# The first stage of a two-layer block on one core: tiles mixed in two pairs and kept in SBUF, two rows broadcast by TensorE

## The reference, cut to what matters

```python
def first_block(...):
    sh1, sc1, g1, sh2, sc2, g2 = split(silu(c) @ ada_w + ada_b)      # 1024 -> 6*1024
    u = rms_norm(x, mix_pre_g) * (1 + sc1) + sh1
    y = concat([(window_mean(u_g, w) - u_g) @ pool_w[g] for g, w in enumerate((2, 4, 8, 16))]) * pool_scale
    x = x + g1 * rms_norm(y, mix_post_g)
    u = rms_norm(x, ffn_pre_g) * (1 + sc2) + sh2
    f = conv_ffn(u, w_up, conv_w, conv_b, w_down)
    return x + g2 * rms_norm(f, ffn_post_g)
```

## Time and profile before

| | us |
|---|---|
| median of three runs | 1283.73 |
| profiled execution, its own time | 1283.86 |
| its span | 1282.0 |
| PE busy | 1216.9 (95% of the span) |
| first product of the up units starts | 93.53 |
| product 49, the first of the second unit, starts | 106.82 |
| DVE, ACT, POOL busy | 551.5, 520.3, 378.6 |

### The profile page before, as it was taken

How to read it: one execution, slowest core, us unless ns; L and a number is a source line. 1 busy time by engine, 2 the same in 40 slices (tenths; PEclk the granted TensorE clock), 3 DMA queues, 4 the chain that set the end, 5 groups by cost and what they waited for, 6 DMA issues and landing times.

```text
span 1282.0 us, 16325 instructions
## 1 busy us (share of the span) xinstructions
PE 1216.9 (95%) x6572; PEld 1019.9 (80%) x6572; DVE 551.5 (43%) x853; ACT 520.3 (41%) x669; POOL 378.6 (30%) x92
## 2 busy tenths in 40 slices
PE   5989999999899989999999999999999699999986
PEld 5568878888788867888788978888888479999874
DVE  1464344343722253558854357422100632453714
ACT  4254543445411145654343324644312544335523
POOL 0014433444434433224221120044444124233111
PEclk9889999999999989999999999999999789999998
DMA  9993223222322232223322112032322313222101
GB/s 352 386 323 106 92 83 98 95 91 90 109 94 99 99 125 73 66 50 116 99 66 67 34 33 99 1 93 72 131 99 99 106 33 99 67 66 67 65 1 66
DMA packets 108206, 128.48 MB, mean 100 GB/s; under 512 B 13019, under 2 KB 98785, under 8 KB 108017
## 3 DMA queue, kind: packets, MB, share of 16 engines
q1 hardware_dynamic: 103412, 120.69, 28.2%
q10 hardware_dynamic: 4733, 6.91, 1.6%
HBM read 122.35 MB, written 5.24 MB: 100 GB/s over the span
## 4 chain that ended last, share of the span: by engine, by line
PE 45%; DVE 3%; ACT 1%; issue 1%; DVEq 0%; ACTq 0%
PE ps L242 11%; PE ps L244 11%; PE ps L243 11%; PE ps L1482 2%; PE ps L2064 2%; PE ps L1821 1%; PE ps L1829 1%; PE ps L1858 1%; PE ps L1949 1%; PE ps L1955 1%; PE ps L1950 1%; PE ps L1931 1%; DVE xres L1377 1%; PE ps L2083 1%; DVE xres L1367 0%
## 5 line engine op out<-in xcount | busy, mean ns | idle before, releaser
L364 POOL TENSOR_TENSOR wl<-raw,wh 128x2048 fp32r<-128x2048 f32 x81 | 374.4, 4622 | 875.3 <-ACT wh L389 875.3
L242 PE MATMUL ps<-xth,wh 128*128 128x512 f32 x800 | 321.2, 401 | 3.9 <-DVE xtl L974 3.2
L244 PE MATMUL ps<-xth,wl 128*128 128x512 f32 x800 | 313.6, 392 | 0.0
L389 ACT ACTIVATE wh<-raw 128x2048 fp32r<-128x2048 f32 x81 | 154.9, 1912 | 390.5 <-PE ps L244 390.5
L243 PE MATMUL ps<-xtl,wh 128*128 128x512 f32 x800 | 313.0, 391 | 0.0
L242 PEld LDWEIGHTS ps<-xth,wh 128*128 128x128 f32 x800 | 151.4, 189 | 36.5 <-issue 6.7
L244 PEld LDWEIGHTS ps<-xth,wl 128*128 128x128 f32 x800 | 151.0, 189 | 32.5
L243 PEld LDWEIGHTS ps<-xtl,wh 128*128 128x128 f32 x800 | 151.6, 190 | 29.1
L242 PE MATMUL ps<-wh,xth 128*128 128x256 f32 (+1 forms) x320 | 98.8, 309 | 3.4 <-DVE xtl L867 3.4
L243 PE MATMUL ps<-wl,xth 128*128 128x256 f32 (+1 forms) x320 | 98.0, 306 | 0.0
L244 PE MATMUL ps<-wh,xtl 128*128 128x256 f32 (+1 forms) x320 | 97.8, 306 | 0.0
(11 more groups left out here) (287 smaller groups left out, 1733.1 us busy)
## 6 DMA issues: line engine op xcount, KB each, us to landing
ada<-in_ada_w SPq DMA_DIRECT2D x24, 1024.0 KB, 10.6
raw<-in_gdn_w_in SPq DMA_DIRECT2D x24, 1024.0 KB, 5.1
raw<-in_ffn_w_up SPq DMA_DIRECT2D x22, 1024.0 KB, 5.0
raw<-in_gla_w_in SPq DMA_DIRECT2D x12, 1024.0 KB, 5.0
raw<-in_ffn_w_down SPq DMA_DIRECT2D x11, 1024.0 KB, 4.8
raw<-in_gdn_w_out SPq DMA_DIRECT2D x8, 1024.0 KB, 4.9
raw<-in_gla_w_out SPq DMA_DIRECT2D x4, 1024.0 KB, 5.0
xres<-in_x SPq DMA_DIRECT2D x4, 512.0 KB, 5.2
```

The source lines that it names most:

```text
L242: nc.tensor.matmul(o, lh, rh, start=first, stop=False)
L244: return nc.tensor.matmul(o, ll, rh, start=False, stop=last)
L364: nc.gpsimd.tensor_tensor(wl[:, s, :], raw[:, s, :], wh[:, s, :].bitcast(f32), ALU.subtract)\
L389: nc.scalar.activation(wh[:, s, :], raw[:, s, :], ACT.Copy).then_inc(hi_done, 1)
```

## The change

- The rows `pool_scale` and `mix_post_g` are loaded to one partition (`scale_rows`, 4 KB each, at the head of SP's program) in place of 512 KB each. PE spreads them with four products of a column of ones (one partition, 512 columns each) into banks 0 to 3, placed after the turned rows and ahead of the band sums; ACT copies them to `pool_scale_row` and `post1_row`, ahead of the squares of x. The first `ada_unit` waits for these copies. The band matrices are stored three times in place of four (864 KB in place of 1152 KB).
- `mixed` takes two tiles at once, the pair 0 and 1 and then the pair 2 and 3; the second pair waits only for ACT's new copy of y to SBUF (`y_copied`), and comes ahead of all four units of group 3.
- ACT's program: for each of the four tiles the squares, the copy and the root of y; then for each tile the squares, root and `xn` of u. DVE's program: `norm` of y no longer adds to x; `mixed_in(tt)` does that from the SBUF copy, with g1. They stand in the order that the diff shows.
- `mod_cols` with scale are computed with the gain multiplied in first.
- ACT makes the high part from `pooled` itself, with scale and shift (Identity), and waits only for `mods_done` and the four turned tiles; DVE computes the same value to a ring of four and subtracts, block by block.
- The first up unit goes block by block, both chunks in each block (`first_unit`): six products for each low part.

```diff
-NORM_ORDER = (("y", 0), ("y", 1), ("u", 0), ("y", 2), ("u", 1), ("y", 3), ("u", 2), ("u", 3))
+NORM_ORDER = tuple((what, tt) for what in "yu" for tt in range(TT))
+BAND_OF = (0, 1, 1, 2)
...
-    pool_band = at("pool_band", PH + 40 * KB, [POOL_GROUPS, TT, BAND])
+    pool_band = at("pool_band", PH + 40 * KB, [POOL_GROUPS, TT - 1, BAND])
+    scale_rows = at("scale_rows", PH + 16 * KB, [2, D])
+    y_early = at("y_early", PH + 24 * KB, [2, D])
+    y_late = at("y_late", PH + 40 * KB, [2, D])
+    u_ring = at("u_ring", PH + 24 * KB, [4, T])
...
+        def y_of(tt):
...
+            return (y_early if tt < 2 else y_late)[:, tt % 2, :]
...
+            sp.dma_start(scale_rows[0:1, 0, :], a["pool_scale"][0].rearrange("(a n) -> a n", a=1)).then_inc(S("ident_in"), 16)
+            sp.dma_start(scale_rows[0:1, 1, :], a["mix_post_g"][0].rearrange("(a n) -> a n", a=1)).then_inc(S("ident_in"), 16)
...
-            sp.dma_start(pool_scale_row[:], a["pool_scale"][0].partition_broadcast(P)).then_inc(S("pool_in"), 16)
...
-            sp.dma_start(post1_row[:], a["mix_post_g"][0].partition_broadcast(P)).then_inc(S("post_in"), 16)
...
+            act.wait_ge(S("rows_turned"), 2)
+            nc.scalar.activation(pool_scale_row[:], bank2(2), ACT.Copy).then_inc(S("c_silu"), 1)
+            nc.scalar.activation(post1_row[:], bank2(0), ACT.Copy).then_inc(S("c_silu"), 1)
...
-            norm_square("y", 0)
-            norm_root("y", 0)
-            norm_square("y", 1)
-            norm_root("y", 1)
-            norm_square("u", 0)
-            norm_square("y", 2)
-            norm_root("u", 0)
-            norm_root("y", 2)
-            norm_square("u", 1)
-            norm_square("y", 3)
-            norm_root("u", 1)
-            norm_root("y", 3)
-            norm_square("u", 2)
-            norm_root("u", 2)
-            norm_square("u", 3)
-            norm_root("u", 3)
+            for tt in range(TT):
+                norm_square("y", tt)
+                nc.scalar.activation(y_of(tt), bank2(4 + 2 * (tt % 2)), ACT.Copy).then_inc(S("y_copied"), 1)
+                norm_root("y", tt)
+            for tt in range(TT):
+                norm_square("u", tt)
+                norm_root("u", tt)
...
+            act.wait_ge(S("mods_done"), 5)
+            act.wait_ge(S("turned_out"), TT)
...
-                act.wait_ge(S("pooled_ready"), KD + k + 1)
-                nc.scalar.activation(xth[:, k, :], pooled[:, k, :], ACT.Copy).then_inc(S("pooled_done"), 1)
+                nc.scalar.activation(xth[:, k, :], pooled[:, k, :], ACT.Identity, scale=mod_cols[:, SC2, k:k + 1],
+                                     bias=mod_cols[:, SH2, k:k + 1]).then_inc(S("pooled_done"), 1)
...
+            for which, gain in ((SC1, PRE1), (SC2, PRE2)):
+                V.scalar_tensor_tensor(cond_cols[:, which, :], cond_cols[:, which, :], 1.0, cond_cols[:, gain, :], ALU.add, ALU.mult)\
+                    .then_inc(S("cols_done"), 1)
+            v.wait_ge(S("cols_done"), 6)
...
-                    V.scalar_tensor_tensor(out, ps[:, b, 0:KD], 1.0, bias, ALU.add, ALU.add).then_inc(S("cols_done"), 1)
-                    v.wait_ge(S("cols_done"), 10 if which == SC1 else 11)
-                    V.tensor_tensor(out, out, cond_cols[:, gain, :], ALU.mult).then_inc(S("mods_done"), 1)
+                    V.tensor_tensor(ps[:, b, 0:KD], ps[:, b, 0:KD], cond_cols[:, gain, :], ALU.mult).then_inc(S("cols_done"), 1)
+                    v.wait_ge(S("cols_done"), 12 if which == SC1 else 13)
+                    V.tensor_tensor(out, ps[:, b, 0:KD], bias, ALU.add).then_inc(S("mods_done"), 1)
...
-                if what == "y":
-                    inv_root(stat[:, 1, tt:tt + 1], D, EPS, count)
-                    y = bank2(4 + 2 * (tt % 2))
-                    V.scalar_tensor_tensor(y, y, stat[:, 1, tt:tt + 1], g1_row[:], ALU.mult, ALU.mult).then_inc(S("scaled"), 1)
-                    own("scaled")
-                    V.tensor_tensor(xres[:, tt, :], xres[:, tt, :], y, ALU.add).then_inc(S("x1_done"), 1)
-                else:
-                    inv_root(stat[:, 2, tt:tt + 1], D, EPS, count)
+                inv_root(stat[:, 1 if what == "y" else 2, tt:tt + 1], D, EPS, count)
...
+            def mixed_in(tt):
...
+                v.wait_ge(S("y_copied"), tt + 1)
+                y = y_of(tt)
+                V.scalar_tensor_tensor(y, y, stat[:, 1, tt:tt + 1], g1_row[:], ALU.mult, ALU.mult).then_inc(S("scaled"), 1)
+                own("scaled")
+                V.tensor_tensor(xres[:, tt, :], xres[:, tt, :], y, ALU.add).then_inc(S("x1_done"), 1)
...
-            v.wait_ge(S("pool_in"), 48)
+            v.wait_ge(S("pool_in"), 32)
+            v.wait_ge(S("c_silu"), 3)
...
-            v.wait_ge(S("cols_done"), 8)
+            v.wait_ge(S("cols_done"), 10)
...
+            norm("y", 0)
...
+            norm("y", 1)
...
-            v.wait_ge(S("post_in"), 16)
...
-            norm("y", 0)
-            norm("y", 1)
+            mixed_in(0)
+            norm("y", 2)
+            norm("y", 3)
+            mixed_in(1)
+            norm("u", 0)
...
-            norm("u", 0)
-            norm("y", 2)
+            mixed_in(2)
...
-            norm("y", 3)
+            mixed_in(3)
+            mod_col(3, 2, SH2)
...
-            mod_col(3, 2, SH2)
...
-                V.tensor_scalar(pooled[:, k, :], pooled[:, k, :], mod_cols[:, SC2, k:k + 1], mod_cols[:, SH2, k:k + 1],
+                V.tensor_scalar(u_ring[:, k % 4, :], pooled[:, k, :], mod_cols[:, SC2, k:k + 1], mod_cols[:, SH2, k:k + 1],
...
-                if k >= 1:
-                    v.wait_ge(S("pooled_done"), 2 * KD + k)
-                    V.tensor_tensor(xtl[:, k - 1, :], pooled[:, k - 1, :], xth[:, k - 1, :].bitcast(f32), ALU.subtract)\
-                        .then_inc(S("u_lo"), 1)
-            v.wait_ge(S("pooled_done"), 3 * KD)
-            V.tensor_tensor(xtl[:, KD - 1, :], pooled[:, KD - 1, :], xth[:, KD - 1, :].bitcast(f32), ALU.subtract).then_inc(S("u_lo"), 1)
+                v.wait_ge(S("pooled_ready"), KD + k + 1)
+                v.wait_ge(S("pooled_done"), 2 * KD + k + 1)
+                V.tensor_tensor(xtl[:, k, :], u_ring[:, k % 4, :], xth[:, k, :].bitcast(f32), ALU.subtract).then_inc(S("u_lo"), 1)
...
-            pe.wait_ge(S("ident_in"), 32)
+            pe.wait_ge(S("ident_in"), 64)
...
-                                  pool_band[:, cb // 2, tt, 0:nc_], start=(tt == 0), stop=(tt == TT - 1), skip_group_check=True)
+                                  pool_band[:, cb // 2, BAND_OF[tt], 0:nc_], start=(tt == 0), stop=(tt == TT - 1), skip_group_check=True)
...
-            def mixed(tt):
...
-                if tt >= 2:
-                    pe.wait_ge(S("x1_done"), tt - 1)
+            def mixed(t0):
...
-                    if tt == 0:
+                    if t0 == 0:
...
-                    for k in range(2):
-                        mm = X.matmul(ps[:, 4 + 2 * (tt % 2) + g // 2, (g % 2) * GDIM:(g % 2 + 1) * GDIM],
-                                      pooled[:, 2 * g + k, tt * P:(tt + 1) * P], pool_w[:, g, k, :], start=(k == 0), stop=(k == 1))
-                mm.then_inc(S("y_mm"), 1)
+                    for tt in (t0, t0 + 1):
+                        if t0 and g == 0:
+                            pe.wait_ge(S("y_copied"), tt - 1)
+                        for k in range(2):
+                            mm = X.matmul(ps[:, 4 + 2 * (tt % 2) + g // 2, (g % 2) * GDIM:(g % 2 + 1) * GDIM],
+                                          pooled[:, 2 * g + k, tok(tt)], pool_w[:, g, k, :], start=(k == 0), stop=(k == 1))
+                        if g == POOL_GROUPS - 1:
+                            mm.then_inc(S("y_mm"), 1)
...
-                    pe.wait_ge(S("x1_done"), 3 + tt)
+                    pe.wait_ge(S("y_copied"), 3 + tt)
...
+            pe.wait_ge(S("prepared"), 6)
+            for r in range(2):
+                for half in range(2):
+                    mm = X.matmul(ps[:, 2 - 2 * r + half, :], ones[0:1, 0:1].broadcast_to([1, P]),
+                                  scale_rows[0:1, r, half * 512:(half + 1) * 512], start=True, stop=True)
+            mm.then_inc(S("rows_turned"), 1)
...
-            pe.wait_ge(S("prepared"), 6)
...
-                    mm = X.matmul(ps[:, 4 + g, c0:c0 + nc_], ones[:, 0:1].broadcast_to([P, P]), pool_band[:, g, tt, 0:nc_],
+                    mm = X.matmul(ps[:, 4 + g, c0:c0 + nc_], ones[:, 0:1].broadcast_to([P, P]), pool_band[:, g, BAND_OF[tt], 0:nc_],
...
+            pe.wait_ge(S("c_silu"), 3)
...
-            pe.wait_ge(S("cols_done"), 8)
+            pe.wait_ge(S("cols_done"), 10)
...
-            pe.wait_ge(S("cols_done"), 9)
+            pe.wait_ge(S("cols_done"), 11)
...
-            mixed(1)
-            ada_unit(3, 0, 0)
-            ada_unit(3, 1, 0)
...
-            ada_unit(3, 2, 0)
-            ada_unit(3, 3, 0)
-            mixed(3)
+            for n in range(4):
+                ada_unit(3, n, 0)
...
+            ada_unit(4, 0, 0)
...
```

(28 more changed lines are left out.)

## The result

The changed kernel took 1293.53 us (median of four, 1291.8 to 1294.02) against 1283.11 for the kernel before (four, 1282.41 to 1283.79): a ratio of 1.0078, 95% interval 1.0061 to 1.0095. It is slower, by 10.4 us. The forecast was 1290.9 with a range of 1285.5 to 1295.0. The profiled execution spans 1292.2 us, 10.2 more than the 1282.0 of before.

What follows compares the result with a forecast made beforehand. PE, 95% busy, was taken as the bound, so the second up unit's start moves the end. First unit's start +6.7 us and the unit itself +0.3 make +7.0: 1283.86 to 1290.9 us, range 1285.5 to 1295.

Steps and rivals of the forecast that it cites:

- Leg 1: Ahead of the mixing: the spread rows start ACT's squares 8.3 us late; `mod_col(1)` is through at 49.7, 4.5 us late.
- half clock after PE's gap: First pool blocks onward: PE's idle and thin stretch to 31.5 brings half clock, costing 1.7 us (0 to 3.4).
- That nothing waits for `ada_w` late: PE before the mixing: the saved 1.3 MB of loads remove its 1.64 us wait for `ada_w`.
- Leg 2: Mixing: each pair of tiles takes 7.4 us; the first pair ends at 59.7, the second at 73.2.
- Leg 3: Tail before the up units: `mixed_in(1)` behind `norm(y, 3)` runs only at 77.1; POOL's low part ends at 99.3.
- PE's cover in the tail: Tail: PE's last turn, `ada` and `mod_col` stay covered by POOL's low part; loss 0, up to 1.5 us.
- Leg 4: First up unit: DVE stands still during POOL's low parts; the unit starts at 100.2, the second at 113.8.
- the hold of DVE by POOL's second low part: Within the first up unit: DVE stands for up to 4.6 us, costing 0.5 us (0 to 1.5).
- PE's lead of 3 to 4 us: First up unit: PE has a lead of some 3 to 4 us while POOL's second low part holds DVE.
- That PE's program is the bound: Rival, 7%: PE's waits of 2.37 and 1.64 us vanish and the first unit runs at full clock; 1281.7 us.
- The small losses: Rival, 15%: they do not add up; row products near full clock, no half clock from the gap; +1.1 to +4 us.
- The half clock of the tail: Rival, 10%: 77 to 105 nearly all at half clock, tail +2 and first unit up to 2 more; 1295 us.

Runs made afterwards that it cites:

- e7: Changed kernel with ACT's two row copies behind the four `xn` and `mixed_in(1)` ahead of the norms of y tiles 2 and 3; ratio 1.0011 to before.
- e2: Changed kernel with only ACT's two copies of the spread rows moved behind the four `xn`; ratio 1.0021 to the kernel before.
- e1: Changed kernel with the two rows again loaded to 128 partitions by SP, without PE's products and ACT's copies; ratio 1.0030 to the kernel before.
- e3: Changed kernel with `mixed_in(1)` right behind `mixed_in(0)`, ahead of the norms of y tiles 2 and 3; ratio 1.0043 to the kernel before.
- e8: Kernel before with early high parts of units 0 and 1, high part straight from ACT, ring of four and block-by-block first unit; ratio 1.0001 to before.
- e4: Changed kernel with ACT's high part of the second up unit held until DVE's eighth low part is there; ratio 1.0073 to the kernel before.
- e6: Kernel before with only ACT's high parts of up units 0 and 1 moved earlier; ratio 1.0001 to the kernel before.

## Why the prediction came out as it did

The direction, the place and the mechanisms held; the sum was short by 3.2 us of 10.2. The change is slower because what it added ahead of ACT's first work and into DVE's order delayed the start of the up units; with both put elsewhere (e7) 8.0 of the 8.6 us are gone.

- *Leg 1* held. Row products 7.19 us where I took 6.4, squares at 21.1 (20.5), fourth `xn` at 32.0 (31.4), half clock after PE's gap, taken at 1.7 us and worth 3.1 (four pool blocks in 7.22 us in place of 4.08): `mod_col(1)` at 50.8 (49.7). e2 shows that the price is ACT's place in line, 4.9 of the 8.6 us. That nothing waits for `ada_w` late held in the changed kernel and not without its saved bytes (2.75 us at 45.53 in e1).
- *Leg 2* held: first pair through at 60.5 (59.7), second at 73.7 (73.2).
- *Leg 3* held: `mixed_in(1)` at 77.3 (77.1), last `xn` through at 93.5 (92.8), POOL's low part at 99.9 (99.3). e3 prices the one misplaced addition at 1.5. PE's cover in the tail, taken as 0, was 0: `mod_cols` was ready at 98.2, before POOL.
- *Leg 4* held in kind and was short in size. Start at 101.0 (100.2), of which 0.6 was brought in from the legs before. The mis-sized term is the hold of DVE by POOL's second low part, taken at 0.5 us with an end of 1.5: the first unit took 14.4 (13.6), though less of it ran at half clock than the 4.4 us assumed (3.6), and without any hold it is 12.9 (e8), so the hold cost 1.5 or a little more. PE's lead of 3 to 4 us was right: when POOL began at 105.84, the five finished blocks lasted PE until 109.66, 3.8 us. What was wrong is what stood against it. A hold of 4.6 us less a lead of 3 to 4 is 0.6 to 1.6 by the prediction's own numbers, not 0.5; and the sixth low part came only at 111.10, 5.3 us after POOL's start (4.71 of POOL and 0.55 of the subtraction behind it).
- *The step that was missing* is 1.6 us after the stage, where the same pause of PE brought a half-clock spell in one profile and not in the other. Its cause stays open. That the time still fell inside the range is not to the prediction's credit here: nothing in it stood for these 1.6 us.
- The rule of the Trainium skill ("SBUF — State Buffer", section "SBUF: two separate sides") that I used held here for 8 columns (1.17 us in e8, until POOL ends) as for 512 (4.97 us, gone in e4 and e8), both with two inputs in SBUF, and not for operations of one column on one tile (0.14 us in e6), which it lists only if they run in a two-port mode. The late `mod_cols` product, which reads PSUM and one SBUF tile and was taken as not stopped, was not (0.17 us at 98.00, under POOL's low part).
- *Rivals.* That PE's program is the bound failed: its wait of 1.64 us for `ada_w` went, but that of 2.37 became one of 4.22 (for ACT's `xn`, at 81.56), and the last `xn` ended 8.5 us later (93.5, before 85.0). The small losses did add up. The half clock of the tail was there (0.50 from 81 to 91) but lay beside DVE's additions.

## What to carry to other kernels

A copy or a wait that goes in ahead of an engine's first work delays that engine's whole chain, even if the producer's time looks hidden (here ACT's squares by 8.9 us and the second unit by 4.9): put it at the latest point that its reader allows. When one engine is freed of another's pace, look at what it will start sooner and which shared resource that takes; here ScalarE's lead served to park GpSimd's low part on top of VectorE's blocks. And a short wait of TensorE ahead of its long run is worth filling with unused products if the granted clock falls there.

## What was not expected of the hardware

- 1.28 us of unused products within a wait of 3 us kept the granted clock at full through the start of the long run, worth 1.9 us in one kernel (first unit 12.9 to 11.0) and 2.5 in another (13.5 to 11.0; its second unit came 1.4 earlier).
- The landing of one small load, 24 KB issued behind 2 MB, decided the start of PE's work in one execution (13.47 in place of 11.08): 2.4 us there, and still 1.95 at `mod_col(1)`.
- The same 3.3 us pause was followed by half clock in ten profiles and by full clock in three.
- Half clock and the hold of VectorE by GpSimd cover each other: the same operation of 4.97 us cost TensorE 1.34 us of idle time with 3.6 us of half clock in the unit, and 0.20 with 6.0.
